# Four 64x512 copies of the GDN solve move from VectorE to ScalarE, and the low half of the output is written behind the solve's last sums

## What is computed

```python
def gated_delta_rule(q, k, v, g, beta):          # chunks of 64 tokens
    decay = jnp.exp(jnp.where(lower, g[..., :, None] - g[..., None, :], -jnp.inf))
    L = jnp.where(strict, jnp.einsum('bhncd,bhnsd->bhncs', kb, k) * decay, 0.0)
    T = lax.linalg.triangular_solve(eye + L, eye, left_side=True, lower=True, unit_diagonal=True)
    u, w = T @ vb, T @ (kb * jnp.exp(g)[..., None])
    def step(state, inp):
        v_new = u_n - w_n @ state
        o = q_n @ state + a_n @ v_new
        state = state * gl_n + k_n.T @ v_new
        return state, o
    ...
def gdn_mixer(h, w_in, conv_w, A_log, dt_bias, norm_w, w_out):
    qkv = jax.nn.silu(causal_depthwise_conv(qkv, conv_w))
    ...
    o = rmsnorm(o, norm_w) * zg
    return o.reshape(B, S, GDN_V_WIDTH) @ w_out
```

## Time and profile before

| | |
|---|---|
| median of three runs | 2735.11 us (2734.95 to 2738.89) |
| the profiled execution | 2736.56 us, of which the traced span is 2734.8 us |
| PE busy | 2681.2 us, 98% of the span |
| DVE, ACT, POOL busy | 1787.3 us (65%), 1274.7 us (47%), 899.6 us (33%) |
| granted clock of PE, mean | 0.998 of full |
| GDN turns | about 1866 to 2400 us of the span; a mid turn takes some 69 us |

### The profile page before, as it was taken

How to read it: one execution, slowest core, us unless ns; L and a number is a source line. 1 busy time by engine, 2 the same in 40 slices (tenths; PEclk the granted TensorE clock), 3 DMA queues, 4 the chain that set the end, 5 groups by cost and what they waited for, 6 DMA issues and landing times.

```text
span 2734.8 us, 40987 instructions
## 1 busy us (share of the span) xinstructions
PE 2681.2 (98%) x15550; PEld 2223.8 (81%) x15550; DVE 1787.3 (65%) x2641; ACT 1274.7 (47%) x2008; POOL 899.6 (33%) x751
## 2 busy tenths in 40 slices
PE   8999999999999999999999999999999999899998
PEld 6998888789888898887788998877777777777777
DVE  7974336569753687635956887348777777676664
ACT  4542232445323453223554543345555555467775
POOL 5520013136431264403733545104422222122232
PEclk9999999999999999999999999999999999999999
DMA  5343332223553325533213256322222222122222
GB/s 144 87 123 93 96 82 78 82 80 101 170 159 94 96 85 157 175 96 85 78 31 90 83 145 181 106 70 71 78 70 70 70 70 63 44 78 65 66 62 70
DMA packets 484876, 255.94 MB, mean 94 GB/s; under 512 B 17843, under 2 KB 478422, under 8 KB 484710
## 3 DMA queue, kind: packets, MB, share of 16 engines
q1 hardware_dynamic: 484534, 253.40, 32.4%
q10 hardware_dynamic: 176, 0.27, 0.0%
HBM read 251.51 MB, written 2.13 MB: 93 GB/s over the span
## 4 chain that ended last, share of the span: by engine, by line
PE 89%; DVE 6%; ACT 2%; issue 1%; POOL 1%; DMA 0%; SPq 0%; DVEq 0%; ACTq 0%; POOLq 0%
PE bank L281 60%; PE bank L978 12%; PE bank L2495 1%; PE bank L2526 1%; PE bank L2528 1%; DVE w_lo L267 1%; PE bank L2527 1%; DVE dsa_work L2191 1%; PE bank L3435 1%; PE bank L3427 1%; DVE small L2185 1%; PE bank L2640 1%; PE bank L3460 1%; DVE gdn_blocks L3030 1%; PE bank L1569 1%
## 5 line engine op out<-in xcount | busy, mean ns | idle before, releaser
L267 DVE TENSOR_TENSOR w_lo<-w_raw,w_hi 128x1024 fp32r<-128x1024 f32 x365 | 463.1, 1271 | 463.2 <-ACT w_hi L261 443.8
L281 PE MATMUL bank<-x_hi,w_hi 128*128 128x512 f32 x1808 | 737.7, 408 | 6.0 <-DVE w_lo L267 4.2
L281 PE MATMUL bank<-x_lo,w_hi 128*128 128x512 f32 x1808 | 707.8, 391 | 0.6 <-DVE x_lo L623 0.6
L281 PE MATMUL bank<-x_hi,w_lo 128*128 128x512 f32 x1808 | 707.5, 391 | 0.0
L261 ACT ACTIVATE w_hi<-w_raw 128x1024 fp32r<-128x1024 f32 x349 | 366.9, 1056 | 489.7 <-PE bank L281 440.7
L281 PEld LDWEIGHTS bank<-x_hi,w_hi 128*128 128x128 f32 x1808 | 340.4, 188 | 88.1 <-issue 16.5
L281 PEld LDWEIGHTS bank<-x_hi,w_lo 128*128 128x128 f32 x1808 | 340.1, 188 | 74.3
L281 PEld LDWEIGHTS bank<-x_lo,w_hi 128*128 128x128 f32 x1808 | 341.1, 189 | 68.1 <-DVE x_lo L623 3.9
L468 POOL TENSOR_TENSOR sumsq<-sumsq,sq 128x512 f32<-128x512 f32 x56 | 90.3, 1613 | 711.8 <-ACT sq L456 711.2
L281 PE MATMUL bank<-h_hi,w_hi 128*128 128x512 f32 x768 | 300.3, 391 | 0.0
L281 PE MATMUL bank<-h_hi,w_lo 128*128 128x512 f32 x768 | 299.0, 389 | 0.0
(11 more groups left out here) (542 smaller groups left out, 5070.1 us busy)
## 6 DMA issues: line engine op xcount, KB each, us to landing
w_raw<-in_ffn_wi_dram SPq DMA_DIRECT2D x176, 512.0 KB, 3.8
w_raw<-in_ffn_wo_dram SPq DMA_DIRECT2D x64, 512.0 KB, 3.5
w_raw<-in_ada_w_dram SPq DMA_DIRECT2D x48, 512.0 KB, 4.8
w_raw<-in_a_w_in_dram SPq DMA_DIRECT2D x48, 512.0 KB, 4.0
w_raw<-in_b_w_in_dram SPq DMA_DIRECT2D x32, 512.0 KB, 4.0
w_raw<-in_ffn_wo_dram SPq DMA_DIRECT2D x32, 384.0 KB, 3.1
w_raw<-in_even_w_in_dram SPq DMA_DIRECT2D x16, 512.0 KB, 4.0
w_raw<-in_a_w_out_dram SPq DMA_DIRECT2D x16, 512.0 KB, 3.5
```

The lines of the kernel that those rows point to most:

```text
L267: dve.tensor_tensor(w_lo[s][:], w_raw[raw_of(b) % RAW][:], w_hi[s][:].bitcast(F32), ALU.subtract).then_inc(w_lo_done, 1)
L281: mm = pe.matmul(out, lhs[:, w], rhs(kt), start=first and kk == 0 and m == 0, stop=last and kk == len(kts) - 1 and m == 2)
```

## The change

`ga`, `gb`, `f2b` and `at` become ScalarE copies: `ga` and `gb` directly behind `fa` and `fb`, `f2b` between `f2a` and `c`, `at` directly in front of `ct`. PE's waits follow: f2 now waits for `gb` of ScalarE alone, v for `hb` of VectorE and `f2b` of ScalarE, vn0 for `ct` of ScalarE alone. VectorE waits for `gb` before `ha` and `hb`. On VectorE `low` moves from in front of `va` and `vb` to behind them. PE's own order is the same.

```diff
             act = Steps(...)
-            ["kc", "vc_0", "vc_1", "fa", "fb", "f2a", "c", "y", "bt", "ct"]
+            ["kc", "vc_0", "vc_1", "fa", "fb", "ga", "gb", "f2a", "f2b", "c", "y", "bt", "at", "ct"]
             dve = Steps(...)
-            ["P", "PT", "ga", "gb", "ha", "hb", "f2b", "va", "vb", "at"]
+            ["P", "PT", "ha", "hb", "va", "vb"]
...
 # gdn_pe
                 beside("c")
-                act("fb")
-                dve("gb")
+                act("gb")
                 halves("f2", ...)
                 beside("f2")
-                act("f2a")
-                dve("f2b")
+                dve("hb")
+                act("f2b")
                 halves("v", ...)
...
-                dve("at")
                 act("ct")
...
 # gdn_act
                 run("fb", G.F[b, :], first(1)[b], ACT.Copy)
+                pe("g")
+                run("ga", G.m[a, :], second(0)[a], ACT.Copy)
+                run("gb", G.m[b, :], second(1)[b], ACT.Copy)
                 splits("f")
                 pe("f2")
                 run("f2a", G.F2[a, :], first(0)[a], ACT.Copy)
+                run("f2b", G.F2[b, :], first(1)[b], ACT.Copy)
                 run("c", G.CY[a, :], first(0)[b], ACT.Copy)
...
                 pe("at")
+                run("at", G.T[a, :, a], halves(first(0)[a]), ACT.Copy)
                 run("ct", G.T[a, :, b], halves(first(1)[a]), ACT.Copy)
...
 # gdn_dve
                 pe("g")
-                for n, r, src in (("ga", a, second(0)), ("gb", b, second(1))):
-                    dve.tensor_copy(G.m[r, :], src[r]).then_inc(*done(n))
+                act("gb")
                 for n, r, src in (("ha", a, second(0)), ("hb", b, second(1))):
                     tt(n, halves(G.V1[r, :]), halves(src[r]), eye(r), ALU.add)
-                pe("f2")
-                dve.tensor_copy(G.F2[b, :], first(1)[b]).then_inc(*done("f2b"))
                 splits("vc")
-                if p is not None:
-                    low(p)
                 pe("v")
                 own("hb")
                 for n, r, src in (("va", a, second(0)), ("vb", b, second(1))):
                     tt(n, G.V[r, :], G.V1[r, :], src[r], ALU.add)
+                if p is not None:
+                    low(p)
                 splits("f")
...
-                pe("at")
-                dve.tensor_copy(G.T[a, :, a], halves(first(0)[a])).then_inc(*done("at"))
```

More of the change, by code:

```diff
@@ L2389, in first_and_second_block @@
                        + ["sums"])
-            act = Steps(sem("gdn_act"), ["kc", "vc_0", "vc_1", "fa", "fb", "f2a", "c", "y", "bt", "ct"]
+            act = Steps(sem("gdn_act"), ["kc", "vc_0", "vc_1", "fa", "fb", "ga", "gb", "f2a", "f2b", "c", "y", "bt", "at", "ct"]
                         + [n for t in range(TT) for n in both([f"vn{t}"])] + both(["sq", "oc"]))
             dve = Steps(sem("gdn_dve"), both(["m", "in", "E", "at"]) + [f"{n}{k}" for k in range(GDN_STEPS) for n in ("ta", "tb")]
-                        + ["P", "PT", "ga", "gb", "ha", "hb", "f2b", "va", "vb", "at"]
+                        + ["P", "PT", "ha", "hb", "va", "vb"]
                         + [n for t in range(TT) for n in (both([f"r{t}"]) if t else []) + (both([f"s{t}"]) if t < TT - 1 else [])])
```

## The result

The median went from 2736.19 us (2734.95 to 2738.89, 19 runs) to 2742.16 us (2739.32 to 2744.07, 19 runs). The ratio is 1.0019, with a 95% interval of 1.0013 to 1.0025: 5 to 6 us slower, just inside the 0.2% that were taken as no change, and outside the range. The profiled execution took 2742.86 us with a span of 2741.1, which is 6.3 us more than before.

The account below looks back on a forecast made before the run. TensorE was taken as busy nearly all of the span, so only its waits count. The terms -7.1 - 1.8 + 0.8 + 2.2 + 1.5 = -4.4 us, from 2735.11, gave 2730.7 us, range 2727.8 to 2734.5.

Parts of the forecast that it names:

- What is late next: `low` itself: Mid turns, VectorE: `low` can start about 2089.8 and ends by 2091.1 as before; k's convolution starts no later behind y.
- the part on `low` behind the sums: Mid turns: with `low` moved behind `va`, `vb`, TensorE's wait at y is gone, 1.8 us gained.
- the slower rival: Mid turns: ScalarE's queue, behind k's late convolution, makes vn0 wait; 6 x 1.8 = 10.8 us, 2741.5 us; chance 0.09.
- x: How much later ScalarE's chain to vn0 comes against TensorE than worked out; TensorE waits x minus 0.8 us per mid turn.
- one of the signs that the prediction named for being wrong: Wrong if: a wait at v or at vn0 in the mid turns, or a last turn that loses nothing.
- The last turn's stall: Last turn: moved `low` makes `O0` start at 2364.8 instead of 2362.58, 2.2 us lost; TensorE stands some 2.8 us.
- The term for the clock: Last turn: longer waits cause one drop to the 1.2 GHz level, 1.5 us lost, bounds 0 and 2.5.
- the waits at f2 and y: Mid turns: f2's waits shrink from 7.6 to 0.5 us, 7.1 gained; y's wait goes, 1.8 gained.
- `v10` as the cover of `f2b`: Mid turns: product `v10` between f2 and v hides ScalarE's second copy of F2, no cost, 0.15 us to spare.
- the second copy on the path and `ct` late: First turn: v 0.5 us later for F2's second copy, vn0 0.4 to 0.5 later for `at`; 0.8 us lost taken.
- the three waits of the last turn: Last turn: TensorE's waits of 1.55, 0.89 and 1.16 us become about 1.7, 1.4 and 2.8 us.
- the prediction's first rival: Last turn: no drop of the clock, as it can miss in some executions; sum -5.9, 2729.2 us; chance 0.22.

Follow-up runs that it names:

- the whole with two repairs: Changed kernel with GpSimd's four decay-row additions started later in the mid turns and `low` before `va`, `vb` in the last turn alone: 2729.47 us, ratio 0.9975.

## Why the prediction was wrong

The profiled execution came out 10.7 us above the forecast sum of -4.4: 8.3 in the six mid turns (0.6 gained instead of 8.9), 1.85 in the last turn (5.55 lost instead of 3.7) and 0.76 ahead of the stage; the first turn lost 0.2 less than forecast.

**The failed step** is "What is late next: `low` itself" in the part on `low` behind the sums. It said that `low` ends by 2091.1 as before, and that the convolution of k "starts no later behind y than before". `low` did start where I put it, 5.30 us behind f2 (2090.76 - 2085.46; forecast 2089.8 - 2084.52 = 5.28); but it took 2.38 us, the `w_lo` behind it 2.30, and the convolution came 2.1 us later behind y. What I left out is an engine: `vb` releases GpSimd too, and I moved an operation past that release without asking what the release starts. Before, one `w_lo` was all that met the additions, and there GpSimd was the one that waited: its first pair took 3.57 us, in the later start 2.54. Over the six turns `low` is longer by 6.5 us and `w_lo` by 5.8 than where the additions start later. The groups of VectorE in the mid turns (busy time, mean ns of one) show it; the changed kernel:

```profile
L267 DVE TENSOR_TENSOR w_lo<-w_raw,w_hi 128x1024 fp32r<-128x1024 f32 x48 | 64.0, 1354 | 35.9 <-ACT w_hi L261 35.8
L3023 DVE TENSOR_TENSOR gdn_o_lo<-gdn_sq,gdn_o_hi 128x512 fp32r<-128x512 f32 x12 | 14.3, 1235 | 0.2
```

And the changed kernel with the additions started later:

```profile
L267 DVE TENSOR_TENSOR w_lo<-w_raw,w_hi 128x1024 fp32r<-128x1024 f32 x48 | 58.2, 1221 | 39.5 <-ACT w_hi L261 39.3
L3023 DVE TENSOR_TENSOR gdn_o_lo<-gdn_sq,gdn_o_hi 128x512 fp32r<-128x512 f32 x12 | 7.8, 689 | 0.2
```

The rest of the chain is the slower rival's: a late convolution, then silu of k, the squares, `at`, `ct`, and TensorE at `vn0`. I had that chain with x below zero and a chance of 0.09. Its place was right, and with x as measured its size too, but its cause was another: the lateness came from VectorE's lengthened operations, not from one more copy on ScalarE. With x at 2.1 us, that rival takes 2.1 - 0.8 = 1.3 us from each mid turn, 7.8 in six; `vn0` came 1.27 us later behind y, and 8.3 us are missing. (Its 6 x 1.8 goes with x = 2.6, not 2.5.) The listed waits are 0.6 us at `vn0`, 0.3 at `O1` and 0.2 behind it; with 0.3 us more busy time of TensorE (67.49 against 67.20) they used up the gain of each turn without turning it into a loss. The wait at `vn0` in the mid turns is one of the signs that the prediction named for being wrong.

**The last turn's stall was right, its clock mis-sized.** From f to the end the turn lost 5.55 us where 2.2 + 1.5 were forecast. At `O0` the loss was 3.69 - 0.75 = 2.94 (2366.27 against 2362.58), of which v's longer matmuls at the low clock are 0.64 (1.79 against 1.15); the remaining 2.3 answer to the forecast of 2.2. The term for the clock is then 0.64 + (5.55 - 2.94) = 3.2 us instead of 1.5, and beyond its bound of 2.5, because the low level lasted 10.1 us and not 3.4. I priced it after a single wait of the first turn; here three waits follow one another. With the same waits at f2 and v and a shorter one at `O0`, the experiments stood 6.8 us (wait of 0.49) or 3.4 us (wait of 1.32) at the low level, so the length of the last wait alone doesn't set it. The 3.2 us are those of one execution: the mean granted clock of the nineteen ran from 0.994 to 0.998, with 0.994 in the profiled one and 0.996 in the median one. And the prediction took from the earlier trace rows that the waits of the kernel before leave the clock at full; a run below shows that they needn't.

**Right:** the waits at f2 and y and what they are worth (1.41 us a turn once nothing else interferes); `v10` as the cover of `f2b` in the mid turns, with no wait at v; in the first turn the second copy on the path and `ct` late, 0.6 against 0.8; the three waits of the last turn. In the first and last turn, where nothing covers the second copy, v waited 1.36 and 1.35 us instead of 0.85 and 0.89.

## What to carry to other kernels

Before an operation is moved past a semaphore's signal, list every engine that waits for this signal and what each starts then: the moved operation will run beside that work. VectorE's instructions that read two tiles from SBUF and GpSimd's elementwise work are best placed apart, and such work with slack can be released by an instruction with one such input, as here a convolution that reads a bank. A change of two parts is to be priced in halves: here the one part was worth about nothing, the other cost 12 us, and the whole with two repairs gained 7.

## What the runs showed of the hardware

VectorE and GpSimd hold each other up by most of an instruction of the other: by some 1.1 us, where one addition alone takes 1.3 us and one `w_lo` 1.22. In the mid turn after, the second `low` took 1.78 us instead of 0.69, `w_lo` 2.30 instead of 1.22, and GpSimd's additions 2.0 instead of 1.0 where `w_lo` stood before them; the convolution, with one input in a bank, took 0.75 us beside the same additions. The Trainium skill ("SBUF — State Buffer", section "Who interferes with whom") says that the two engines share one pair of ports as an exclusive lock, that a VectorE instruction with two SBUF inputs contends for it with a GpSimd instruction that reads SBUF, that one with at most one such input, outside VectorE's 2-port modes, does not, and that the order of issue decides which of the two blocks. The traces agree in all of these cases.

After the same two waits of 1.69 and 1.35 us at f2 and v the low level of the clock lasted 10.1 us with a wait of 2.87 us behind them (10.2 in the run with the additions later, with the same three waits), 6.8 us with one of 0.49 and 3.4 us with one of 1.32. What decides between them stays open; it was not tested.

The same instructions, after the same waits, can also meet either level. In the last turn of the run with the additions earlier, whose code there is that of the kernel before, f2 and v waited 1.55 and 0.89 us as in the earlier trace rows, and yet the clock fell there, while it stayed at 1.00 in the earlier trace rows:

```profile
2370.56 1.84 PE L2495 MATMUL bank<-gdn_W,gdn_W 64*64 64x64 f32 x32 [0.89 <-DVE gdn_W L3096]
```

```profile
2370.80:2374.20 3.40, 2.93 (x34) 2.57 (x31) 2.66 (x4) 2.11 (x4) 0.00 (x0) 0.50 0.00 0
```

And in the first turn of the run with the additions later, with the code of the changed kernel, TensorE waited 1.65 us in front of f instead of 2.19, and the clock did not fall:

```profile
1880.00:1896.00 16.00, 12.91 (x207) 10.20 (x205) 12.51 (x24) 8.44 (x13) 4.50 (x4) 1.00 0.14 38
```

So a drop can come or miss from one execution to the next, as the prediction's first rival supposed, and the length of a low stretch in one profiled execution is not shown to be the price of the waits in front of it.
